# Gate and value products of four feed-forwards: rows of tokens, 512 columns wide, in place of turned tiles 256 wide

## The reference: what is computed

```python
g, wg, wu, wd = ffn1[layer]                       # wg, wu: 1024 x 2816; wd: 2816 x 1024
h = h + 0.5 * swiglu(rmsnorm(h, g), wg, wu, wd)   # swiglu(x, ...) = (silu(x @ wg) * (x @ wu)) @ wd
```

## Time and profile before

| | |
|---|---|
| Median of three runs | 1744.34 us |
| Profiled execution, its time | 1746.13 us |
| Its span, first to last instruction | 1744.6 us |
| Mean granted clock of TensorE | 0.966 of full speed |
| TensorE matmul, busy | 1649.4 us, 95% |
| VectorE, busy | 1064.6 us, 61% |
| ScalarE, busy | 854.0 us, 49% |
| The four changed stages, first matmul on the gates to the first of the down product | 530.90 to 658.51, 977.50 to 1104.50, 1167.24 to 1294.25, 1553.13 to 1680.14 us |

### The profile page before, as it was taken

How to read it: one execution, slowest core, us unless ns; L and a number is a source line. 1 busy time by engine, 2 the same in 40 slices (tenths; PEclk the granted TensorE clock), 3 DMA queues, 4 the chain that set the end, 5 groups by cost and what they waited for, 6 DMA issues and landing times.

```text
span 1744.6 us, 24970 instructions
## 1 busy us (share of the span) xinstructions
PE 1649.4 (95%) x10364; PEld 1481.4 (85%) x10364; DVE 1064.6 (61%) x1549; ACT 854.0 (49%) x1231; POOL 29.4 (2%) x30
## 2 busy tenths in 40 slices
PE   7988987899999999997989999999999999999998
PEld 7877876799979998885767899889998887789997
DVE  4555657589846554576857656455554766765553
ACT  4454645566545443453446544444443555664442
POOL 0000003000000000000000000000000000000000
PEclk9988988999999999998689999999999999999999
DMA  7746324455554545543034455554555541535553
GB/s 280 277 146 232 118 76 145 167 183 188 178 183 152 190 174 193 188 173 121 1 117 149 173 190 182 184 189 171 192 183 179 193 145 73 175 115 179 184 193 121
DMA packets 42975, 290.20 MB, mean 166 GB/s; under 512 B 5048, under 2 KB 5198, under 8 KB 9968
## 3 DMA queue, kind: packets, MB, share of 16 engines
q1 hardware_dynamic: 38272, 271.93, 43.4%
q0 software_dynamic: 4592, 16.69, 2.8%
HBM read 287.51 MB, written 8.55 MB: 170 GB/s over the span
## 4 chain that ended last, share of the span: by engine, by line
PE 87%; DVE 5%; ACT 3%; DMA 2%; issue 1%; DVEq 1%; POOL 1%; POOLq 0%; SPq 0%; ACTq 0%
PE bank L451 26%; PE bank L453 25%; PE bank L452 25%; PE bank L457 6%; PE bank L716 2%; DMA raw<-stream_dram 2%; DVE low L419 1%; PE bank L1466 1%; PE bank L603 1%; ACT high L408 1%; DVEq L2376 1%; POOL xn L1405 0%; PE bank L1664 0%; DVE u L962 0%; DVE h L1083 0%
## 5 line engine op out<-in xcount | busy, mean ns | idle before, releaser
L408 ACT ACTIVATE high<-raw 128x2048 fp32r<-128x2048 f32 x257 | 489.1, 1914 | 547.3 <-DMA raw<-stream_dram 537.6
L419 DVE TENSOR_TENSOR low<-raw,high 128x2048 fp32r<-128x2048 f32 x255 | 582.6, 2291 | 259.8 <-ACT high L408 258.5
L451 PE MATMUL bank<-xh,high 128*128 128x256 f32 x1880 | 534.2, 284 | 1.1 <-DVE low L419 1.1
L452 PE MATMUL bank<-xl,high 128*128 128x256 f32 x1880 | 532.9, 283 | 0.0
L453 PE MATMUL bank<-xh,low 128*128 128x256 f32 x1880 | 532.8, 283 | 0.0
L451 PEld LDWEIGHTS bank<-xh,high 128*128 128x128 f32 x1880 | 362.1, 193 | 2.1 <-issue 2.1
L452 PEld LDWEIGHTS bank<-xl,high 128*128 128x128 f32 x1880 | 361.9, 193 | 0.0
L453 PEld LDWEIGHTS bank<-xh,low 128*128 128x128 f32 x1880 | 361.8, 192 | 0.0
L451 PE MATMUL bank<-high,xh 128*128 128x512 f32 (+2 forms) x528 | 207.6, 393 | 6.7 <-DVEq L2376 4.3
L452 PE MATMUL bank<-low,xh 128*128 128x512 f32 (+2 forms) x528 | 204.0, 386 | 0.0
L453 PE MATMUL bank<-high,xl 128*128 128x512 f32 (+2 forms) x528 | 203.9, 386 | 0.0
(11 more groups left out here) (229 smaller groups left out, 1550.3 us busy)
## 6 DMA issues: line engine op xcount, KB each, us to landing
raw<-stream_dram SPq DMA_DIRECT2D x257, 1024.0 KB, 4.8
band_wide_dram<-band_rows_dram POOLq DMA_DIRECT2D x1, 3072.0 KB, 28.8
t_wide_dram<-t_rows_dram POOLq DMA_DIRECT2D x1, 2304.0 KB, 15.4
u<-mem_dram POOLq DMA_DIRECT2D x2, 1024.0 KB, 5.2
bias<-band_wide_dram POOLq DMA_DIRECT2D x1, 2048.0 KB, 14.1
rel_wide_dram<-rel_rows_dram POOLq DMA_DIRECT2D x1, 1920.0 KB, 17.2
bias<-t_wide_dram POOLq DMA_DIRECT2D x1, 1536.0 KB, 8.0
bias<-rel_wide_dram POOLq DMA_DIRECT2D x1, 1280.0 KB, 7.0
```

The source lines that it names most:

```text
L408: act.activation(self.high[:, n % RING, :], self.raw[:, n % RING, :], ACT.Copy).then_inc(self.high_split, 1)
L419: dve.tensor_tensor(self.low[:, n % RING, :], self.raw[:, n % RING, :], self.high[:, n % RING, :].bitcast(F32), ALU.subtract).then_inc(sel ...
L451: pe.matmul(out, lh, rh, start=start, stop=False)
L452: pe.matmul(out, lh, rl, start=False, stop=False)
```

## The change

The four feed-forwards without convolution become a new stage, `RowFfn`. The operands trade places: a block of 128 tokens of `xh` or `xl` is stationary, and the weights are moving, 512 wide: 256 columns of `wg` beside the same 256 of `wu`. The work goes in 11 chunks of 256 hidden features. A chunk has 8 pieces (two slots), and each piece takes 3 matmuls for each of two blocks of tokens: 48 matmuls 512 wide. A bank then holds tokens on partitions, 256 gates and 256 values. The stream holds the same numbers in as many slots, in another order.

With tokens on partitions, ScalarE takes silu straight from the bank with the factor of the norm as its scale, and VectorE multiplies by the values: 128 x 256 each, for each block. The product has to be turned for the down product: 4 turnings for each chunk (`turn_chunk`), 44 in a stage, issued in the middle of the next chunk (the last one's in the down product). ScalarE rounds the turned bank to `hh` and VectorE subtracts for `hl`, 128 x 512 at a time. `inv_row` and its turnings are not needed in these stages.

```diff
-        plan += [(f"up1_{layer}", FT * 2 * KT, P), (f"down1_{layer}", 2 * FT, HALF)]
+        plan += [(f"up1_{layer}", FT * KT // 2, HALF), (f"down1_{layer}", 2 * FT, HALF)]
...
+    def sides(g, u):
+        g, u = by_chunk(g, S), by_chunk(u, S)
+        return [np.concatenate(two, 1) for two in zip(g, u)]
...
-            pieces[f"up{n}_{layer}"] = pairs(g(f"ffn{n}_wg"), g(f"ffn{n}_wu"))
+            pieces[f"up{n}_{layer}"] = sides(g(f"ffn{n}_wg"), g(f"ffn{n}_wu"))
...
+class RowFfn(Ffn):
+    CHUNKS = FT // 2
+    def __init__(self, core, up, down, source, factor=1.0, **options):
+        super().__init__(core, up, down, source, factor, **options)
+        work = core.square[:, :, :].rearrange("p a b -> p (a b)")
+        part = lambda at: work[:, at:at + 2 * HALF].rearrange("p (n b w) -> p n b w", n=2, b=NB)
+        self.gate_rows, self.product_rows = part(0), part(2 * HALF)
+    def sums(self, c, b):
+        return self.core.bank[2 * (c % 2) + b]
+    def turned(self, c):
+        return self.core.bank[4 + c % 2 if c < self.CHUNKS - 1 else 2][:, :]
+    def turn_chunk(self, pe, s, c):
+        pe.wait_ge(s["gates_ready"], 2 * c + 2)
+        if c >= 2:
+            pe.wait_ge(s["hidden_ready"], c - 1)
+        for j in range(2):
+            for b in range(NB):
+                at = j * S + b * P
+                last = pe.transpose(self.turned(c)[:, at:at + P], self.product_rows[:, c % 2, b, j * P:(j + 1) * P],
+                                    self.core.ident)
+        last.then_inc(s["tiles_turned"], 1)
+    def tensor(self, pe, s):
+        core = self.core
+        self.rows.tensor(pe, s)
+        for c in range(self.CHUNKS):
+            if c >= 2:
+                pe.wait_ge(s["gates_ready"], 2 * c - 2)
+            for k in range(KT):
+                if c == 0:
+                    self.rows.arrive(pe, s, k)
+                i = c * KT + k
+                w = core.piece(pe, self.up, i)
+                for b in range(NB):
+                    last = mm3(pe, self.sums(c, b)[:, :], (core.xh[:, k, block_cut(b)], core.xl[:, k, block_cut(b)]), w,
+                               k == 0, k == KT - 1)
+                    if k == KT - 1 and b == 0:
+                        last.then_inc(s["banks_filled"], 1)
+                core.release(last, self.up, i)
+                if k == KT // 2 - 1 and c:
+                    self.turn_chunk(pe, s, c - 1)
+        pe.wait_ge(s["hidden_ready"], self.CHUNKS - 1)
+        Residual.tensor(self, pe, s)
+    def input_wait(self, pe, s, k):
+        if k == 1:
+            self.turn_chunk(pe, s, self.CHUNKS - 1)
+        pe.wait_ge(s["hidden_ready"], k // 2 + 1)
+    def scalar(self, act, s):
+        core = self.core
+        self.rows.scalar(act, s)
+        core.split_high(act, self.up.first)
+        act.wait_ge(s["inverse_ready"], 1)
+        for c in range(self.CHUNKS + 1):
+            core.split_high(act, self.up.first + 2 * c + (1 if c < self.CHUNKS else 0))
+            if c:
+                act.wait_ge(s["tiles_turned"], c)
+                act.activation(core.hh[:, 2 * c - 2:2 * c, :].rearrange("p n q -> p (n q)"), self.turned(c - 1), ACT.Copy)\
+                   .then_inc(s["highs_ready"], 1)
+            if c < self.CHUNKS:
+                for b in range(NB):
+                    if b:
+                        act.wait_ge(core.slot_used, self.up.slot(c * KT + KT - 1) + 1)
+                    else:
+                        act.wait_ge(s["banks_filled"], c + 1)
+                        if c >= 2:
+                            act.wait_ge(s["gates_ready"], 2 * c - 2)
+                    act.activation(self.gate_rows[:, c % 2, b, :], self.sums(c, b)[:, 0:S], ACT.Silu,
+                                   scale=core.inv[:, 2 + b:3 + b]).then_inc(s["inputs_ready"], 1)
+        Residual.scalar(self, act, s)
+    def vector(self, dve, s):
+        core = self.core
+        self.rows.lows(dve, s)
+        core.split_low(dve, self.up.first + 1 - LEAD)
+        self.rows.vector_norms(dve, s, self.factor)
+        core.split_low(dve, self.up.first)
+        for c in range(self.CHUNKS + 1):
+            core.split_low(dve, self.up.first + 2 * c + (1 if c < self.CHUNKS else 0))
+            if c:
+                dve.wait_ge(s["highs_ready"], c)
+                cut = (slice(None), slice(2 * c - 2, 2 * c))
+                dve.tensor_tensor(core.hl[cut].rearrange("p n q -> p (n q)"), self.turned(c - 1),
+                                  core.hh[cut].rearrange("p n q -> p (n q)").bitcast(F32), ALU.subtract)\
+                   .then_inc(s["hidden_ready"], 1)
+            if c < self.CHUNKS:
+                for b in range(NB):
+                    dve.wait_ge(s["inputs_ready"], 2 * c + b + 1)
+                    if c >= 2:
+                        dve.wait_ge(s["tiles_turned"], c - 1)
+                    dve.tensor_tensor(self.product_rows[:, c % 2, b, :], self.gate_rows[:, c % 2, b, :],
+                                      self.sums(c, b)[:, S:HALF], ALU.mult).then_inc(s["gates_ready"], 1)
...
-        st.append(Ffn(c, f"up1_{layer}", f"down1_{layer}", rows(l + "_ffn1"), factor=0.5))
+        st.append(RowFfn(c, f"up1_{layer}", f"down1_{layer}", rows(l + "_ffn1"), factor=0.5))
```

More of the change, by code:

```diff
@@ L200, in stream_plan @@
         plan += [(f"wq{layer}", KT, HALF), (f"wkv{layer}", 2 * KT, HALF), (f"wo{layer}", 8, HALF)]
-        plan += [(f"up2_{layer}", FT * 2 * KT, P), (f"down2_{layer}", 2 * FT, HALF)]
+        plan += [(f"up2_{layer}", FT * KT // 2, HALF), (f"down2_{layer}", 2 * FT, HALF)]
     out, first = {}, 0
@@ L1240, in vector @@
                 c.split_low(dve, self.up.first + step + 1)
+        Residual.vector(self, dve, s)
+class RowFfn(Ffn):
[87 more added lines that the diff above has]
+                                      self.sums(c, b)[:, S:HALF], ALU.mult).then_inc(s["gates_ready"], 1)
@@ L2356, in stages_of @@
         after = [(c.bias[:, 0:16, :], toeplitz(dram["band_wide"], 16))] if layer == 0 else []
-        st.append(Ffn(c, f"up2_{layer}", f"down2_{layer}", rows(l + "_ffn2"), factor=0.5,
+        st.append(RowFfn(c, f"up2_{layer}", f"down2_{layer}", rows(l + "_ffn2"), factor=0.5,
                       loads=Loads(*after) if after else None,
```

## The result

The changed kernel takes 1749.6 us (median of 20 runs, 1741.8 to 1753.1) against 1743.6 us before, also over 20 runs. By the medians that is 6.0 us more. The ratio on record is 1.0025, 95% interval 1.0014 to 1.0037, which is 4.4 us (2.4 to 6.5 us): slower by a quarter of a per cent. The forecast was 1735 us. Its profiled execution took 1747.4 us, with a span of 1745.6 us and a mean granted clock of 0.958 (before: 0.966).

A forecast was written before the change was run, and what follows sets the result against it. TensorE, busy for 95% of the span, was taken as the bound, by its matmul count times pace. Wider matmuls, added turnings and removed turnings summed to -8.5 us, 1735.8 us for the median, set to 1735 us; range 1728 to 1745 us.

The forecast's parts named there:

- Paces: Gates and values product, changed stages: 512-wide matmuls at 0.2268 us against 0.2400 for two narrow ones, -6.97 us a stage.
- The rule on the gap: Skill's 262 and 518 cycles for 256 and 512 columns: matmuls only -1.3 us a stage, whole slower by 13 us.
- Turnings: Changed stages: 0.44 us for each group of four, 11 groups, +4.84 us a stage; the removed two give -0.21 us.
- Cover by ScalarE and VectorE: Inside each chunk: both engines are free before its end, and the last product has 4.4 us spare before its turning.
- The wait at the down product: Rival at the down product's start: it waits for the tenth chunk's `hl`, 0.3 us a stage, 1.2 us; chance 0.08.
- The sum: Four changed stages: -2.34 us each, -9.4 us together, or -7.6 us at the slower projection period; middle -8.5 us.
- The clock: Rival behind the first changed stage: half-clock stretches may move, adding or taking some 5 us, 1730 or 1740 us; chance 0.07.

## Why the prediction was wrong

*Paces.* Right. 0.2277 us for the wide matmul against bounds of 0.2268 and 0.2400; it took the projections' slower pace in all chunks, which the prediction had as the smaller end of the gain.

*The rule on the gap.* The product with gates and values fell by 2.4 us a stage with the turnings in it, 127.00 to 124.61 us. By the figures of the Trainium skill (TensorE: Matmul & The Clock Gate, Back-to-back issue gap), two narrow matmuls cost 2.5 ns more than a wide one, and by an estimate from this the product would have grown; the measurement decides.

*Turnings.* Right: 0.44 us for four, 11 groups in a stage, none with idle time ahead of it.

*Cover by ScalarE and VectorE.* Right. Silu takes 475 ns from the bank where 403 were assumed, with no effect.

*The wait at the down product.* Named, priced at 0 to 1.2 us, taken as 0; it was 0.2 us in one stage of four. The estimate of 0.1 to 0.3 us for a stage with a late transfer was too low as a bound: 1.0 us in the profile with only the first stage changed. It came in the first changed stage in three of the seven profiles that have this stage in the new form (0.2, 0.3 and 1.0 us), and never in the other stages.

*The sum.* -8.5 us was forecast for the stages, -7.6 us is what they gave.

*The clock.* This is the step that failed. The prediction wrote that the stretches at half clock "may begin and end elsewhere" and that this "can add or take some 5 us", with a chance of 0.07, as if each run drew it anew. The place was right and the rest was not. The price is 9 us in the profile and 10 to 14 by the medians, two to three times as much, and more than the whole gain. In the sum it stood at nothing. And it isn't drawn anew: with the mixer tied to the clock's moments, moving it by 1.7 us put most runs on the bad side. For the runs without a profile only the mean clock tells: it is 0.955 to 0.959 in 16 of the 20 (0.958 in the profiled one) and 0.961 to 0.963 in the other four, which took 1741.8 to 1745.9 us. The kernel before with a mere delay shows the same loss, in all five of its runs (1754.4 to 1757.5 us). Why the clock falls for longer at some distances and not at others stays open; the runs show that a shift of the mixer brings the loss, and that the new form is not needed for it. The evidence was in the trace: a stretch of 44 us at half clock that ended inside a stage in which TensorE was the busiest engine. The end of such a stretch is an event on which 11 us hang, and I read only its mean clock.

## What to carry to other kernels

Find the stages where TensorE runs at half clock although it is busy, and price what it would cost if the clock came back later there, before pricing a change of a few us anywhere ahead of them. When a change's own stages show the forecast gain and the total doesn't, compare unchanged stages start by start, and test with a pure delay: a kernel that gets faster when work is added has its answer in the clock. An operand order that is 512 wide pays here even with four turnings for each 48 matmuls, by 1.9 us in 190.

## What the runs showed of the hardware that was not expected

The moments of the granted clock, which I took as chance, hold to the program within 0.5 us at one place (4.3 to 4.8 us behind the stage's start in twelve profiles) while that place itself moves by 9.3 us between them. The masked attention took 57.8 us with the clock back 29.5 us after its start, and 69.2 us when it came back only at its end, with the same instructions. A delay of 1.8 us cost 12.3 us in one kernel and gave 8.1 us in the other.
